# Local attention: probabilities normalised on GpSimd ahead of the transposes, scores of 384 keys in three banks, the memory products in sixteen halves

## The reference

```python
def window_gqa(q, k, v, sinks):      # 16 query heads, 4 key heads, blocks of 128 queries
    # a block of 128 queries sees the 384 keys of its own and its two neighbour blocks (256 at either end)
    scores = einsum(q, k) * 64 ** -0.5, masked to |distance| <= 128
    m = maximum(max(scores), sink)
    p = exp(scores - m)
    probs = p / (sum(p) + exp(sink - m))
    return einsum(probs, v)

kv = rms_norm(mem) @ w_mem_kv[l]      # for both layers l: keys and values of 256 memory rows, 4 heads of 128
x = x + concatenate([window_gqa(...), memory_attention(mq, mk, mv)]) @ w_out[0]
```

## Time and profile before

| | |
|---|---|
| median of 3 runs | 3211.76 us (3211.11 to 3211.96) |
| the profiled execution's own time | 3211.97 us |
| its span | 3210.2 us |
| PE busy | 3160.4 us, 98% of the span |
| DVE, ACT, POOL busy | 56%, 36%, 13% |
| granted PE clock | 0.998 of full speed |
| the stretch of the change | 106.20 to 261.37 us of the span |

### The profile page before, as it was taken

The page is one execution under the profiler, slowest core; times in us unless marked ns, Lnnn a source line. Parts: engine busy times, 40 slices in busy tenths (PEclk is TensorE's granted clock), DMA queues, the critical chain, the costliest instruction groups (busy, mean ns, idle before and its releaser), DMA issues. The chain is left out here.

```text
span 3210.2 us, 41446 instructions
## 1 busy us (share of the span) xinstructions
PE 3160.4 (98%) x15754; PEld 2584.8 (81%) x15754; DVE 1786.2 (56%) x1932; ACT 1143.9 (36%) x1331; POOL 430.5 (13%) x335
## 2 busy tenths in 40 slices
PE   8999999999999999999999999999999999999998
PEld 6778888877788888888877888888888877878887
DVE  7875635459653445534586754345444577664344
ACT  4553212259332222322343433223322343533221
POOL 0002000110100025000253120003000154120002
PEclk9999999999999999999999999999999999999999
DMA  4212232322122224232221122324223221122222
GB/s 158 83 47 99 92 105 92 107 96 83 69 92 92 95 101 122 89 108 92 92 80 66 62 89 86 105 90 131 92 92 104 79 92 67 53 94 93 102 94 76
DMA packets 46600, 293.45 MB, mean 91 GB/s; under 512 B 5888, under 2 KB 6272, under 8 KB 18336
## 3 DMA queue, kind: packets, MB, share of 16 engines
q1 hardware_dynamic: 44496, 286.97, 25.9%
q0 software_dynamic: 2000, 5.05, 1.0%
HBM read 289.24 MB, written 2.10 MB: 91 GB/s over the span
## 5 line engine op out<-in xcount | busy, mean ns | idle before, releaser
L1925 DVE TENSOR_TENSOR w_lo<-w_raw,w_hi 128x2048 fp32r<-128x2048 f32 (+1 forms) x284 | 667.0, 2349 | 244.1 <-ACT w_hi L1484 243.9
L903 PE MATMUL ps<-xg_hi,w_hi 128*128 128x512 f32 x1920 | 749.6, 390 | 2.2 <-DVE w_lo L1925 2.2
L903 PE MATMUL ps<-xg_hi,w_lo 128*128 128x512 f32 x1920 | 747.1, 389 | 0.0
L903 PE MATMUL ps<-xg_lo,w_hi 128*128 128x512 f32 x1920 | 747.0, 389 | 0.0
L1484 ACT ACTIVATE w_hi<-w_raw 128x2048 fp32r<-128x2048 f32 (+1 forms) x286 | 541.1, 1892 | 461.2 <-PE ps L903 359.5
L903 PE MATMUL ps<-hid_hi,w_hi 128*128 128x512 f32 x1216 | 473.3, 389 | 0.0
L903 PE MATMUL ps<-hid_lo,w_hi 128*128 128x512 f32 x1216 | 473.0, 389 | 0.0
L903 PE MATMUL ps<-hid_hi,w_lo 128*128 128x512 f32 x1216 | 473.0, 389 | 0.0
L903 PEld LDWEIGHTS ps<-xg_hi,w_hi 128*128 128x128 f32 x1920 | 360.4, 188 | 79.2 <-issue 4.8
L903 PEld LDWEIGHTS ps<-xg_lo,w_hi 128*128 128x128 f32 x1920 | 360.5, 188 | 75.8 <-issue 1.4
L903 PEld LDWEIGHTS ps<-xg_hi,w_lo 128*128 128x128 f32 x1920 | 360.4, 188 | 75.3
(11 more groups left out here) (369 smaller groups left out, 3902.4 us busy)
## 6 DMA issues: line engine op xcount, KB each, us to landing
w_raw<-up_dram SPq DMA_DIRECT2D x120, 1024.0 KB, 4.8
w_raw<-in_dram SPq DMA_DIRECT2D x42, 1024.0 KB, 4.9
w_raw<-down_dram SPq DMA_DIRECT2D x32, 1024.0 KB, 4.8
w_raw<-down_dram SPq DMA_DIRECT2D x32, 768.0 KB, 4.2
w_raw<-down_dram SPq DMA_DIRECT2D x32, 640.0 KB, 3.9
w_raw<-out_dram SPq DMA_DIRECT2D x14, 1024.0 KB, 4.8
w_raw<-out_dram SPq DMA_DIRECT2D x8, 768.0 KB, 4.2
w_raw<-memk_dram SPq DMA_DIRECT2D x4, 1024.0 KB, 4.9
```

The costliest lines, as they stand in the source:

```text
L903: last = pe.matmul(to, (w_hi, w_lo)[wp][:, q, t:t + P], parts[xp], start=(k == 0 and m == 0), stop=(k == p.ktiles - 1 and m == 2))
L1925: dve.tensor_tensor(w_lo[:, q, 0:w], w_raw[:, q, 0:w], w_hi[:, q, 0:w].bitcast(F32), ALU.subtract)\
```

## The change

The program's constants, the PSUM layout and the four engine lists of this stretch change together. `rec` no longer goes through PE and ACT: GpSimd multiplies the probabilities of a unit by `rec` in place, four instructions, and PE waits for that before it transposes. The 3-key scores lie back to back in banks 0 to 2; since heads of both pairs then share bank 1, the fourth piece waits until the first is done. Bank 3 takes the memory products, one half (256 columns, 24 products) a unit in units 1 to 15, the first ahead of unit 0.

```diff
-MEM_UNITS = (0, 3, 7, 8, 11, 12, 15, 16)
-MEM_SPLITS = {0: 2, 3: 3, 8: 4, 11: 6, 12: 7, 16: 8, 17: 9}
-MEM_AHEAD = {11: 5}
-OUT_FILL = {17: (0, 0, 4), 18: (0, 4, 8), 19: (1, 0, 4)}
+WINDOWS = 16
+MEM_SPLITS = {1: 2, 3: 3, 7: 4, 8: 5, 9: 6, 11: 7, 15: 8, 16: 9}
+OUT_FILL = {16: (0, 0, 3), 17: (0, 3, 6), 18: (0, 6, 8), 19: (1, 0, 4)}
...
+            return [pieces[n] for n in (2, 5, 0, 3, 1, 4)]      # score_order, 3 keys
...
+        def normalise(u):                                        # POOL
+            pool.wait_ge(rec_done, u.n + 1)
+            s_ = score_sb(u)
+            for i in range(u.nh):
+                last = pool.tensor_scalar(s_[:, i, :], s_[:, i, :], rec[:, i:i + 1], None, ALU.mult)
+            last.then_inc(norm_done, 1)
...
+        def memory_half(t):                                      # PE
+            n, h = t // 2, t % 2
             s, l, part = MEM_SLAB + n, n // 4, n % 4
+            pe.wait_ge(evac, EV0 + Q * s + Q // 2 * h)
+            to = ps[:, 3, 0:MEM]
...
+                pe.wait_ge(lo_done, MEM_SLAB + 4 * l + 3 + q)    # values: the second slab only at q == 1
...
+                if shared and at_ == 3:                          # scores
+                    pe.wait_ge(s_part, sum(w.nk == 3 for w in SECTIONS["window"][:u.n + 1]))
...
         def turn_probs(u):
-            pe.wait_ge(exp_done, u.n + 1)
-            if u.kind == "window" and u.nk == 3:
-                pe.wait_ge(evac, EV0 + Q * (MEM_SLAB + sum(m < u.n for m in MEM_UNITS)))
+            if u.kind == "window":
+                pe.wait_ge(norm_done, u.n + 1)
+            else:
+                pe.wait_ge(exp_done, u.n + 1)
...
         def weigh_window(u):
-            pe.wait_ge(rec_done, u.n + 1)
...
-                    last = pe.matmul(ps[g * WIN_D:(g + 1) * WIN_D, u.ot_bank, u.ot_col + i * P:u.ot_col + (i + 1) * P],
-                                     rec[:, h:h + 1].to_broadcast([P, WIN_D]), ident[:], start=True, stop=True)
...
+            memory_half(0)                                       # PE attention, ahead of unit 0
             for n, u in enumerate(us):
                 turn_probs(u)
...
-                if n in MEM_UNITS:
-                    memory_slab(MEM_UNITS.index(n))
+                if 1 <= n < WINDOWS:
+                    memory_half(n)
...
             for n, u in enumerate(us):                           # ACT attention
                 if n + 1 < len(us):
                     exponentials(us[n + 1], n + 1)
+                take_turned(u, n)
+                if n in MEM_SPLITS:
...
         def inverse_window(u):                                   # DVE
...
+            if u.n:
+                dve.wait_ge(norm_done, u.n)
             dve.reciprocal(rec[:], den[:]).then_inc(rec_done, 1)

         def finish_window(u):
-            dve.wait_ge(rec_read, u.n + 1)
             dve.wait_ge(o_psum, u.n + 1)
-            dve.tensor_tensor(o, ps[:, u.o_bank, u.o_col:u.o_col + 2 * P], tmp[:, 1, 0:2 * P], ALU.mult).then_inc(o_ready, 1)
+            dve.tensor_copy(u.hi, o).then_inc(o_ready, 1)        # o is now the PSUM view
             dve.wait_ge(o_ready, u.n + 1)
             dve.tensor_tensor(u.lo, o, u.hi.bitcast(F32), ALU.subtract).then_inc(ot_ready, 1)
...
+            inverse_window(us[0])                                # DVE attention
             for n, u in enumerate(us):
+                if n + 1 < WINDOWS:
+                    inverse_window(us[n + 1])
                 if n + 2 < len(us):
                     front(us[n + 2], n + 2)
...
+                if n < WINDOWS:
+                    memory_half(n)
                     finish_window(u)
```

More of the change, by code:

```diff
@@ L360, in program @@
     s_ready = sem("s_ready")
+    s_part = sem("s_part")
     s_read = sem("s_read")
@@ L576, in score_ps @@
     def score_ps(u):
+        if u.wide and u.nk == 3:
+            return ps[:, 0:3, :].rearrange("p b k -> p (b k)").rearrange("p (g h k) -> p g h k", g=2, h=2)
         if u.wide:
@@ L817, in near @@
                 inv_root(NCB * l + j)
+        for u in SECTIONS["window"][:WINDOWS]:
+            normalise(u)
         for p in PHASES:
@@ L986, in memory_slab @@
                 pe.wait_ge(lo_done, s + 1)
[L987 to L994, removed]
+                for k in range(DT):
+                    for m, (wp, xp) in enumerate(TERMS):
+                        at_ = (h * DT + k) * P
+                        last = pe.matmul(to, (w_hi, w_lo)[wp][:, part, at_:at_ + P], (mem_hi, mem_lo)[xp][:, k, :],
+                                         start=(k == 0 and m == 0), stop=(k == DT - 1 and m == 2))
+                last.then_inc(mm_done, Q // 2)
                 return
             m = part - 2
-            pe.wait_ge(lo_done, MEM_SLAB + 4 * l + 4)
             for q in range(2):
+                pe.wait_ge(lo_done, MEM_SLAB + 4 * l + 3 + q)
                 for k in range(4):
-                    kk = 4 * q + k
+                    kk, at_ = 4 * q + k, k * BANK + h * MEM
                     for n_, (wp, xp) in enumerate(TERMS):
-                        last = pe.matmul(ps[:, 6, :], (mem_hi, mem_lo)[xp][:, kk, m * P:(m + 1) * P],
-                                         (w_hi, w_lo)[wp][:, q, k * BANK:(k + 1) * BANK],
+                        last = pe.matmul(to, (mem_hi, mem_lo)[xp][:, kk, m * P:(m + 1) * P],
+                                         (w_hi, w_lo)[wp][:, q, at_:at_ + MEM],
                                          start=(kk == 0 and n_ == 0), stop=(kk == 7 and n_ == 2))
-                if m:
+                if m and h:
                     last.then_inc(mm_done, Q)
-            if not m:
+            if not (m and h):
                 last.then_inc(mv_mm, 1)
@@ L1016, in scores @@
                 pe.wait_ge(rope_done, 10)
-            for i, (bank, col, off, n) in score_order(u):
+            shared = u.wide and u.nk == 3
+            for at_, (i, (bank, col, off, n)) in enumerate(score_order(u)):
                 o, keys = ps[:, bank, col:col + n], u.k[i]
+                if shared and at_ == 3:
+                    pe.wait_ge(s_part, sum(w.nk == 3 for w in SECTIONS["window"][:u.n + 1]))
                 if u.kind == "near":
@@ L1048, in weigh_window @@
         def weigh_window(u):
-            pe.wait_ge(rec_done, u.n + 1)
+            pe.wait_ge(pt_ready, u.n + 1)
             if u.n:
[L1051 to L1054, removed]
-                    last = pe.matmul(ps[g * WIN_D:(g + 1) * WIN_D, u.ot_bank, u.ot_col + i * P:u.ot_col + (i + 1) * P],
-                                     rec[:, h:h + 1].to_broadcast([P, WIN_D]), ident[:], start=True, stop=True)
-            last.then_inc(ot_psum, 1)
-            pe.wait_ge(pt_ready, u.n + 1)
+                pe.wait_ge(ot_ready, u.n)
             for kb in range(u.nk):
```

90 lines of the change are left out of this document (32 added, 58 removed).

## The result

The kernel after takes 3219.66 us (3217.86 to 3220.81, 9 runs) against 3211.96 (3210.29 to 3212.92, 9 runs) for the kernel before: a ratio of 1.0025, 95% interval [1.0015, 1.0035]. It is 7.7 us slower where 7.1 less were forecast, and outside the range. The profiled execution took 3219.24 us with a span of 3217.4, against 3211.97 and 3210.2.

A forecast was written before the change was run, and what follows sets the result against it. PE, busy 98% of the span, was taken as the bound. Removing 19.2 us, adding 3.5 and 8.9 of new waits gave a gain of 6.8, by a layout 7.4, taken as 7.1: 3204.9 us, range 3201.8 to 3210.5.

The forecast's parts named there:

- GpSimd's price: GpSimd's four multiplications by `rec` take 1.75 or 2.2 us a unit, hidden beside the next `front` except in unit 0.
- the margin of 1.6 for three keys: Between scores and turn of a 3-key unit, PE has 11 us of work beside a chain of 9.4: 1.6 spare.
- No PE wait for them after unit 0: Expected sign in the trace: PE waits for GpSimd's multiplications in unit 0 only.
- rival B: Normalise becomes the bound, its instructions waiting for DVE's: 4.5 us for three keys, 1.6 slower, 3213.4; chance 0.11.
- faster: Whole kernel below 3205.3 us, beyond the 0.2% (6.4 us) that can be told from no change; chance 0.58.
- Removed: On PE in the attention: sixteen broadcasts (7.8 us), 9.1 of waits and their tails go; 19.2 us in sum.
- Added work: On PE: key and value halves, one more `first_out` and the fourth score piece's wait add 3.5 us.
- Unit 0's pause: PE idles 5.3 us before turn 0, which now needs `rec` and GpSimd's multiplications and starts near 116.1.
- Other new waits: PE idles 0.9 us at half 1, 0.5 at weigh 1, 0.7 at half 8, 1.4 turning into unit 16.
- The sum: Over the attention, 19.2 us removed, 3.5 added and 8.9 of new waits: a gain of 6.8, taken as 7.1.
- C: GpSimd's first multiplication starts late, lengthening PE's idleness before turn 0; at 5.3 us more, 3209.9; chance 0.04.
- A rule weighed: GpSimd and DVE share ports under an exclusive lock; collisions in the attention were charged nothing, at worst 1.2 us a unit.

The follow-up runs named there:

- the cheap form: The kernel after with a second operation (times 1.0) in GpSimd's multiplication: 3206.55 us, ratio 0.9984 to the kernel before.
- both repaired: The kernel after with two operations in GpSimd's multiplication and 42 products of no use on PE before turn 0: 3204.85 us, ratio 0.9978 to the kernel before.
- without the normalise: The kernel after with only its banks, halves and splits, division made as in the kernel before, nothing on GpSimd: 3214.5 us, ratio 1.0009.
- the first experiment: The kernel before with 65 chained GpSimd instructions on a scratch tile while GpSimd is idle anyway: 3214.09 us in one timed execution.
- the normalise of unit 0 earlier: The kernel after with unit 0's `rec` made before unit 1's `front`, GpSimd's multiplication still with one operation: 3212.39 us, ratio 1.0002 to the kernel before.
- the fastest kernel: The kernel after with two operations in GpSimd's multiplication and unit 0's `rec` made before unit 1's `front`: 3199.5 us, ratio 0.9963 to the kernel before.
- filler products: The kernel after with products of no use on PE, 57 before turn 0, 18 each before turns 5 and 13: 3215.54 us, ratio 1.0016 to the kernel before.

## Why the prediction was wrong

The step that failed is **GpSimd's price**, "four of them with 0.06 overlap 1.75 and 2.2 us ... from above 2.8". It measured 3.63 and 4.91. The row of 0.69 for 512 columns was read for its operation name and width and not for its arguments: its line in the code has two operations, the new one has one, and the trace gives both the same name. My upper bound was a row of the cheap form as well, so the range didn't hold the true value, and the margin of 1.6 for three keys that the prediction itself worked out was overrun by 1.1 (4.91 less 2.2, less 1.6) in the 3-key units. "No PE wait for them after unit 0" therefore fell with it. The prediction names the break-even of rival B, 4.2 us for three keys; 4.91 lies beyond it.

The second failure is an **omission**: no term was given to PE's clock, though a pause of 5.3 us on an engine that is otherwise busy 98% of the time was part of the forecast. It costs 2.1 even with the cheap form (stretches of 148.0 and 145.9), which by itself puts the time at 3206.55, out of "faster"; 5.1 in the kernel after. The trace of the kernel before could have told of it. Far behind the attention it has this stretch, with PE's waits of 1.25 and 0.56 us in it (to 2651.25 and 2652.51):

```profile
2650.00:2660.00 10.00, 8.19 (x87) 6.68 (x88) 9.15 (x11) 5.07 (x3) 10.00 (x7) 0.83 0.23 95
```

The wide products behind them follow each other at 0.43 us and not at 0.23. The trace of the kernel after has waits of 1.3 and 0.6 at that place and a clock of 1.00 there.

The balance, each from a run (stretch, us against before):

| | forecast | measured |
|---|---|---|
| all other steps | -7.1 | -7.1 (both repaired) |
| normalise 3.63/4.91 for 1.75/2.2 | 0 (+1.6 at its bound of 2.8) | +10.9 (3.8 and 7.1) |
| clock behind the pauses | not there | +5.1 (161.9 less 156.8) |
| sum | -7.1 | +8.9 |

By the medians the three lines are -7.1, +10.7 and +4.1, together the 7.7 measured. The shares are from single traces or medians of executions that differ by some us, so they are good to about 1 us.

Point by point, the rest:
- *Removed.* The broadcasts and nearly all waits went. Right in sum. That each of the waits is open to removal by regular halves alone is not: without the normalise others came in their place. The wait before the last turn wasn't shortened by 0.3 (0.88 for 0.89).
- *Added work.* Halves of 3.05 to 3.07 us and 3.14 for the last two (forecast 3.07), scores of three keys 1.60 (1.6). Right.
- *Unit 0's pause.* 5.3 forecast, 5.5 with the cheap form, 7.3 as the change was made. Right but for the price of the normalise.
- *Other new waits.* Half 8 waits 0.8 (0.7); half 1 0.6 in the kernel after and 0.3 and 0.9 in the two with the cheap form that leave unit 0's `rec` in its place (0.9); weigh 1 0.3 (0.5). The 1.4 before unit 16 didn't come; the 1.1 at the first product of the next phase (L920) is no new one, since the kernel before has it too (1.09 at 268.19, L903).
- *The sum.* Its new waits add up to 8.8 where it has 8.9. With the 1.4 gone the gain by the sum would have been over 8; both repaired gave 7.1. So the other terms were some 1.1 to 1.3 short. Found are the last wait (0.3), some 0.15 of a tail behind each of three new waits, unit 0's pause, 5.6 from the end of half 0 (0.3), and the last two halves (0.1). That the sum came out to the tenth is in part luck.
- *Rivals.* B's sign (PE waits for GpSimd in most 3-key units, five of eight) and its place were right, the normalise as the bound of the chain, its reason wrong: I had it wait for DVE's passes, while it was slow by itself; at 0.11 it had too little. C fell: the first instruction started 0.11 us behind DVE's reciprocal (114.50 and 0.18 long, to 114.79). The clock was no rival at all.
- *A rule weighed.* Nothing charged for the shared ports. Right at this load: in the trace with both repairs no instruction of DVE in the stretch took over 0.05 us longer than the shortest of its shape, in the kernel after two did, 0.5 us together. GpSimd kept busy throughout cost 2.5 in the first experiment. The row of 1.21 is the negation of the four maxima (L2136), not a maximum.

## What to carry over

When a cost is taken from a neighbouring row, compare the instruction's arguments in the code and not its name and width alone: the profile called a one-operation and a two-operation instruction the same, and they differed by a factor of three a column. A pause of PE can have a second price, the slower work behind it (1.4 to 2.5 us each time here), so the long pauses of a layout are to be listed with what runs right after them. And ask of a pause what it waits for in another engine's order: here one call moved ahead of a `front` took the longest one away.

## What the hardware showed that was not expected

- GpSimd's TENSOR_SCALAR with one operation: 2.5 ns a column (930, 1244 and 1566 ns for 256, 384 and 512); with a second operation, a multiplication by 1.0: 0.84 (481, 587, 695). The scalar in the instruction gives 851 for 256, a TENSOR_TENSOR with the scalar broadcast 614, a copy 399. The Trainium skill (GPSIMD Engine Reference, "Elementwise — side-by-side cycle accounting") has bodies of up to two operations bound by the ports at 1.03 cycles an element, which at its 1.2 GHz is an estimate of 0.86 ns: the two-operation form agrees with 0.84, the one-operation form does not, and there the measurement decides.
- PE's granted clock fell from 1.00 to 0.50 behind pauses of 5.5 and 7.3 us, at 2.1 (a difference of two runs) and 2.5 us (from the trace) lost. The length of a pause alone doesn't tell whether it falls. It did behind 3.50 (1.4 lost) and 2.33 (1.6) with the normalise of unit 0 earlier, behind 2.32 twice in the kernel after (1.5 and 1.6), behind 2.08 without the normalise (1.5) and behind 1.91 in the fastest kernel (1.5). It did not behind 2.96 (the first experiment, 151.86), 2.62 (the kernel after, turn 2), 2.40 (without the normalise), 2.34 (with filler products, turn 2) and 2.32 (unit 0 earlier, turn 5). What decides isn't known. Filler products in the pause kept it at 1.00 through the stretch in both profiled executions that had them.
